# Block 1: other PSUM banks for values, gates and the second half of the heads, convolution taps moved out of the k and v tiles; block 2: five score banks in the second layer, output weights of the last head moved

## What is computed

```
def first_block(x, ...):
    h = rms_norm(x, norm1_g)
    glu_in, q, k, v, gate_logits = jnp.split(h @ w_in, SPLITS, axis=-1)
    a_val, a_gate = jnp.split(glu_in, 2, axis=-1)
    a = causal_depthwise_conv(a_val * sigmoid(a_gate), conv_w, conv_b)      # 31 taps
    y_a = silu(rms_norm(a, conv_norm_g)) @ w_conv_out
    q, k = rms_norm per head, q * HEAD_DIM ** -0.5
    o = attention over three dilated windows, mixed by their lse             # per head
    g_a, g_b = split(sigmoid(gate_logits + gate_b))
    x = x + (g_a * y_a + g_b * (o @ w_attn_out)) @ w_out
    u_val, u_gate = split(causal_depthwise_conv(rms_norm(x, norm2_g) @ w_up, ffn_conv_w, ffn_conv_b))
    return x + (silu(u_gate) * u_val) @ w_down

def second_block(x, ...):        # layer a, then layer b
    y = dsa_mixer(x, ...)            # top-k sparse attention with an index, rope, silu gate
    x = layer_norm(ALPHA * x + y)
    y = stick_breaking_mixer(x, ...) # attention weights from a cumulative log product, silu gate
    return layer_norm(ALPHA * x + y)
```

## Time and profile before

| what | value |
|---|---|
| time, median of 3 runs | 1525.65 us (1523.75 to 1526.76) |
| the profiled execution | 1525.49 us, of which its span is 1523.7 us |
| PE busy | 1484.3 us, 97% of the span |
| DVE, ACT, POOL busy | 1068.1, 752.8 and 572.9 us (70%, 49%, 38%) |
| mean granted clock of PE | 0.996 of full speed |
| HBM traffic | 94 GB/s over the span |

### The profile page before, as it was taken

One profiled execution on the slowest core, in us unless ns is written; L12 is line 12 of the kernel. 1 busy time (PEld: TensorE's weight loads), 2 busy tenths in 40 slices (PEclk: granted clock), 3 DMA queues, 4 the chain that ended last, 5 costly groups with the idle time before them and its releaser, 6 DMA issues.

```text
span 1523.7 us, 19634 instructions
## 1 busy us (share of the span) xinstructions
PE 1484.3 (97%) x7070; PEld 1239.2 (81%) x7070; DVE 1068.1 (70%) x1858; ACT 752.8 (49%) x1490; POOL 572.9 (38%) x453
## 2 busy tenths in 40 slices
PE   9999999899999999999999999999998999999998
PEld 8788887787878888888888788878887888888886
DVE  6847689888955567727745646997997451877975
ACT  6566633665263444424423444346776234566750
POOL 2733347664331111111121111565554355444342
PEclk9999999999999999999999999999999999999999
DMA  6455314642234333333333255366662436545522
GB/s 230 119 158 141 108 56 131 166 133 67 85 95 157 95 111 97 98 96 97 97 97 93 82 154 148 111 177 153 163 162 80 166 114 172 156 113 137 137 81 115
DMA packets 74049, 188.58 MB, mean 124 GB/s; under 512 B 10720, under 2 KB 16224, under 8 KB 73696
## 3 DMA queue, kind: packets, MB, share of 16 engines
q1 hardware_dynamic: 73952, 187.33, 43.3%
HBM read 137.48 MB, written 6.29 MB: 94 GB/s over the span
## 4 chain that ended last, share of the span: by engine, by line
PE 80%; DVE 14%; ACT 4%; issue 1%; POOL 1%; DMA 0%; DVEq 0%; SPq 0%; POOLq 0%; ACTq 0%
PE bank L697 18%; PE bank L699 18%; PE bank L698 18%; PE bank L710 5%; PE bank L712 5%; PE bank L711 5%; DVE bank L1326 2%; PE bank L739 2%; DVE p L1315 2%; PE bank L728 2%; PE bank L747 1%; PE bank L729 1%; PE bank L746 1%; ACT p L1137 1%; DVE ptl L1262 1%
## 5 line engine op out<-in xcount | busy, mean ns | idle before, releaser
L1730 POOL TENSOR_TENSOR wlo<-raw,whi 128x512 fp32r<-128x512 f32 x325 | 438.6, 1358 | 866.1 <-ACT whi L949 865.7
L697 PE MATMUL bank<-xh,whi 128*128 128x512 f32 x1000 | 397.6, 398 | 1.9 <-ACT gb L1041 1.9
L949 ACT ACTIVATE whi<-raw 128x512 fp32r<-128x512 f32 x466 | 281.1, 621 | 222.8 <-PE bank L699 140.9
L699 PE MATMUL bank<-xh,wlo 128*128 128x512 f32 x1000 | 390.9, 391 | 0.0
L698 PE MATMUL bank<-xl,whi 128*128 128x512 f32 x1000 | 390.2, 390 | 0.0
L699 PEld LDWEIGHTS bank<-xh,wlo 128*128 128x128 f32 x1000 | 188.0, 188 | 41.1
L697 PEld LDWEIGHTS bank<-xh,whi 128*128 128x128 f32 x1000 | 188.0, 188 | 38.5 <-ACT gb L1041 2.1
L698 PEld LDWEIGHTS bank<-xl,whi 128*128 128x128 f32 x1000 | 188.4, 188 | 37.1 <-issue 0.5
L1326 DVE SCALAR_TENSOR_TENSOR bank<-cbuf,vec,bank 128x512 f32<-128x512 f32 x240 | 164.3, 746 | 20.1 <-ACT bank L974 10.6
L710 PE MATMUL bank<-whi,xh 128*128 128x512 f32 x340 | 135.3, 398 | 3.6 <-DVE ptl L1262 1.5
L711 PE MATMUL bank<-wlo,xh 128*128 128x512 f32 x344 | 134.7, 392 | 0.0
(11 more groups left out here) (251 smaller groups left out, 2660.2 us busy)
## 6 DMA issues: line engine op xcount, KB each, us to landing
raw<-wst SPq DMA_DIRECT2D x224, 512.0 KB, 3.6
stack<-tmpr SPq DMA_DIRECT2D x152, 128.0 KB, 2.4
stack<-fresh SPq DMA_DIRECT2D x64, 128.0 KB, 2.3
stack<-turnr SPq DMA_DIRECT2D x40, 128.0 KB, 2.4
u<-bias SPq DMA_DIRECT2D x16, 256.0 KB, 2.9
rows<-scratch SPq DMA_DIRECT2D x8, 512.0 KB, 8.5
raw<-wst SPq DMA_DIRECT2D x8, 384.0 KB, 3.1
xr<-xt SPq DMA_DIRECT2D x8, 256.5 KB, 5.8
```

The lines of the kernel that those rows point to most:

```text
L697: e.matmul(bank[:, :], h[:, c], a, start=g + i == 0, stop=False)
L699: m = e.matmul(bank[:, :], l[:, c], a, start=False, stop=g + i == nk - 1)
L949: e.activation(whi[k % NHL][:, 0:n], raw[u % NRAW][:, c:c + n], ACT.Copy).then_inc(*WHI.tick(k))
L1730: e.tensor_tensor(wlo[k % NHL][:, 0:n], raw[u % NRAW][:, c:c + n], whi[k % NHL][:, 0:n].bitcast(F32), ALU.subtract).then_inc(*WLP.tick(k))
```

## The change

Block 1. `PK0` and `PK4` move the transposes Pk0 one step later among the first v tiles and Pk4 one step earlier among the second ones. A table `FIXED` takes the place of the rings for the fourth tile of v0, for q1, k1, v1, the gates 9 to 15 and 0 and for Pq6, Pk6, Pq7, Pk7. `conv_plan` gives no tap to the steps of v1 until Pk4, so that 15 taps come later; from there on the later pairs end and start later as well: the copies out of pair 2,3 and the start of pair 4,5 move from the last v1 tile and gate 8 to gates 10, and 16 more taps than before are still to be done when the first `ao` tile begins. In the steps of k1 and v1 the taps stand behind the step's other work on DVE.

Block 2. The transposes of head 15 take the banks of head 14's, the output tiles take other banks, and the fourth output tile's first piece moves behind head 15's transposes. In layer b scores and transposes share five banks (2, 3, 4, 5, 7) instead of four, and the tiles of q, k and gates two (0, 1) instead of three.

```
-PQ0, PK0, PQ4, PK4 = 2, 4, 3, 6
+PQ0, PK0, PQ4, PK4 = 2, 5, 3, 5
...
-SCORE_BANKS = {"": ((4, 2, 3), (4, 2, 3)), "a": ((2, 3, 4, 5, 7), (2, 3, 4, 5, 7)), "b": ((2, 3, 4, 5), (2, 3, 4, 5))}
-TILE_BANKS = {"a": (0, 1), "b": (0, 1, 7)}
+SCORE_BANKS = {"": ((4, 2, 3), (4, 2, 3)), "a": ((2, 3, 4, 5, 7), (2, 3, 4, 5, 7)), "b": ((2, 3, 4, 5, 7), (2, 3, 4, 5, 7))}
+TILE_BANKS = {"a": (0, 1), "b": (0, 1)}
...
+        o0[3:8] = o0[4:7] + o0[3:4] + o0[7:8]
...
+FIXED = {("v0", 3): 0, ("gate", 9): 0, ("Pq", 6): 1, ("gate", 10): 0, ("Pk", 6): 1, ("gate", 11): 1, ("Pq", 7): 0, ("gate", 12): 1,
+         ("Pk", 7): 0, ("gate", 13): 0, ("gate", 14): 1, ("gate", 15): 0, ("gate", 0): 1, **{(name, tb): b for name, bs in (("q1", (0, 1, 4, 2)), ("k1", (3, 6, 0, 1)), ("v1", (4, 2, 3, 6)))
+                         for tb, b in enumerate(bs)}}
...
+            if name[0] == "T" and len(name) == 2 and x[1] == HEADS - 1:
+
+                bank[x] = bank[name, HEADS - 2, x[2]]
+                continue
...
-                used = [bank.get((t, 15, u)) for u in range(3)] + [bank[g, 7]]
-                if None in used:
-                    r = SCORE_BANKS[x[0][1]][0]
-                    used[:3] = [r[(heads + u) % len(r)] for u in range(3)]
+                used = [bank[t, HEADS - 2, u] for u in range(3)] + [bank[g, 7]]
...
+            quota = 0 if second_pairs <= i < PLAN.index(("Pk", 4)) else quota
...
-            for n in CONV_AT.get(step, ()):
-                conv_tap(n)
+
+            if name not in ("k1", "v1"):
+                for n in CONV_AT.get(step, ()):
+                    conv_tap(n)
...
+            if name in ("k1", "v1"):
+                for n in CONV_AT.get(step, ()):
+                    conv_tap(n)
```

More of the change, by code:

```diff
@@ L335, in banks_in_order @@
             now, ring, n = want, rings[want], 0
+        if key in FIXED:
+            bank[key] = FIXED[key]
+            continue
         bank[key] = ring[n % len(ring)]
@@ L350, in conv_plan @@
     first, second = PLAN.index(("q1", 0, 0, 4)), PLAN.index(("gate", GATES[0], 0))
-    third = PLAN.index(("ao", 0, 0))
+    third, second_pairs = PLAN.index(("ao", 0, 0)), PLAN.index(("v1", 0, 0, 4))
     at, n = {}, 0
```

## The result

| | time, us |
|---|---|
| before | 1526.20 median of 4 runs (1523.75 to 1527.19) |
| changed | 1514.65 median of 4 runs (1511.68 to 1515.82) |
| ratio | 0.9925, 95% interval 0.9912 to 0.9937 |
| predicted | 1511.5, range 1507.5 to 1519 |
| profiled execution of the changed kernel | 1513.99, its span 1512.2 |

The change makes the kernel 0.75% faster, 11.5 us by the medians and 11.5 us by the two profiled executions. The forecast was 14.0 us. So direction and range held, and the forecast was 2.5 us too large. The page of the changed kernel answers to the earlier trace rows: PE does the same work in a shorter span, and the chain that ended last is PE's and VectorE's as before.

The account below looks back on a forecast made before the run. The prediction took PE, busy 97% of the span, as the bound, with only idle and low-clock time to win. Place terms of 12.6 us, restarts 0.8 and small gaps 0.6 made 14.0: 1525.5 to 1511.5 us, range 1507.5 to 1519.

Parts of the forecast that it names:

- where the taps go: Gates 10 and 11 and the convolution's sums: deferred taps cost 0.15 of wait and 0.2 of delay, together -0.35 us.
- both waits go: Head 0: with v0's fourth tile in bank 0, waits of 1.30 and 1.20 us go; 2.5 us gained.
- (b): Pk4: without nine taps the k scales end at 250.2, ahead of Pk4's turn at 252.6; 1.94 us gained.
- (e): Pk5: its 0.34 us wait behind ScalarE's two copies of the finished convolution pair goes, as they move to gate 10.
- (f): Gate 9: its 1.85 us wait for a bank shrinks to 0.3 with bank 0; 1.55 us gained.
- (d): S8,0: its 0.95 us wait for k's stack goes, as 9.0 us of PE work covers 8.8 from Pk4.
- (h): T8: waits 2.0 us (0.9 to 2.9) for GpSimd's scaling of head 8, 1.0 more than before; the new limiter.
- (c): Behind Pk4's wait, 262 to 266 us: the granted clock of 0.57 goes with that wait; 1.7 us gained.
- (g): Around T8, 283 to 287 us: the second stretch of granted clock at 0.57 goes; 1.3 us gained.
- Rival (1): Heads 8 on: waits go but the clock falls once, at T8; costs 1.3 to 1.7 us, giving 1513; chance 0.20.
- the prediction's own sign of being wrong: Wrong if sum(1) waits microseconds for DVE, k scales end after Pk4's turn, or the clock is low where it was not.
- Rival (3): At sum(1): 16 deferred taps push the convolution's sums; at 1.75 us a tap +16.5 us, 1528; chance 0.03.

Follow-up runs that it names:

- the moved load: The changed kernel with one 512 KB weight load issued behind the first four of Pk4's stack copies instead of ahead of them; 1517.22 us, ratio 0.9939.
- the banks alone: The kernel before with only layer b's banks changed: five for scores and transposes, two for the tiles; 1526.33 us, ratio 1.0002.
- the stretch alone: The kernel before with only the heads 8 on part: banks of q1, k1, v1 and gates, taps out of v1, Pk4 one step earlier; 1520.54 us, ratio 0.9955.
- the front alone: The kernel before with only v0's fourth tile in bank 0 and Pk0 one step later; 1524.92 us, ratio 0.9993.
- the first four experiments: The first four follow-ups, whose ratios are to the kernel before at 1526.89 us (29 runs).
- head 8's scaling: The changed kernel with one weight load behind Pk4's copies, and head 8's reciprocal and GpSimd's scaling one step earlier; 1514.72 us, ratio 0.9928.
- the last one: The changed kernel with six taps pulled forward, sum(1) and head 8's GpSimd scaling earlier, a weight load later, variance ahead of a low piece; 1510.66 us, ratio 0.9899.

## Why the prediction was right, and where it was off

The direction, the range and most of the waits were right. That the total came within 2.5 us of the forecast is partly luck: in the trace, places forecast too high (head 0, the heads from 8 on, the taps) and a fall of the clock that no term had come to 4.9 us, and 2.2 us that no term had either came in at Sa0,1. Gains by place, with the prediction's eight restarts and 0.6 us of small gaps put where they belong:

| place | forecast, us | measured, us |
|---|---|---|
| head 0 | 2.7 | 1.3 |
| head 7 | 0.6 | 0.4 |
| heads 8 on, to T8 | 7.65 | 6.7 |
| T8 to spread(1), where the taps go | -0.35 | -1.8 |
| Sa0,1 | nothing | 2.2 |
| fall of the clock in layer a | nothing | -1.1 |
| the rest of block 2 | 3.4 | 3.8 |
| sum | 14.0 | 11.5 |

- **Head 0.** The step "both waits go" holds for bank 4. What was missed is who is late next: the prediction watched only the first gate tile and its bank, and not S0,1, which waited 0.38 for a low part of v on the same VectorE.
- **Head 7.** The wait is 0.6 shorter (0.91 for 1.51), as forecast; 0.4 of it is left between the two rows of the table.
- **Heads 8 on.** (b) holds: Pk4 had no wait; the scales ended at 252.8 instead of 250.2, near the bound, and Pk4 stood at 254.16. (e) and (f) hold: Pk5 and gate 9 have no wait. **(d) failed**: "9.0 covers 8.8" took the copies' time for fixed. PE's own work from Pk4 to S8,0 is 9.0 us, as worked out (262.92 - 253.92 with the moved load), but with Pk4 earlier the copies ran into the weight loads: 11.65 us from Pk4 to S8,0, with 5.2 us for a copy where 2.4 had been. This cost 1.0 us at T8. With the moved load the stretch gives 84.9 - 77.2 = 7.7 us, the sum that was forecast. (h), T8 with 2.0 us, was not to be seen in this trace, but 2.05, 1.74, 2.05 and 2.05 us stood there in the four executions in which S8,0 waited less than 1 us. So T8 was the limiter that (h) named: of 2.9 us won back at S8,0, 1.2 arrived behind T8.
- **The clock** ((c) 1.7 and (g) 1.3 us) was a cost in name only. The two falls stood inside the waits for the copies and for the scaling: without them PE waited 2.55 at S8,0 and 2.26 at T8 in the same code, and came to T8 after the same 84.9 us. The sum comes out all the same, since (d) and (h) were worked out with the falls taken off, so that 0.95 + 1.7 is the wait for the copies and 0.96 + 1.3 that for the scaling. What failed is the reading that a fall seen behind a wait is a price of its own, and that it goes with the wait.
- **Where the taps go** (0.35 of loss): 1.5 at sum(1) and spread(1), 0.2 ahead of them. The adds ended one piece of work too late (0.63 of wait), as the upper bound had it. spread(1)'s doubled wait was not in the sum at all. It comes from VectorE's queue, in which the deferred taps push two low parts of weights ahead of the variance: it started at 428.37, over 2 us behind the end of sum(1) (426.23). With the taps given back it came 0.5 us behind that end and spread(1) waited 0.76; with the variance ahead of the low piece, taps deferred, spread(1) didn't wait.
- **Block 2.** The output tiles of layer a gave 1.8 us, the heads of layer b 1.6, the end 0.3. The two edits were costed as independent; the banks alone gave nothing.
- Rival (1), the waits go and the clock still falls, is what happened, and the prediction's own sign of being wrong, a low clock in stretches where it was not, came true at 266 and at 1152 us. The rival had the place and the price wrong: at T8, 2.05 us of wait were followed by a granted clock of 1.00 in the stretch alone; the fall behind S8,0 was mostly hidden, and the one in layer a cost 1.1 to 1.6. The Trainium skill, "TensorE: Matmul & The Clock Gate" (A second HAM failure mode: psum-queue depth-cycling), tells of short idles between groups that make the clock swing. The traces agree in that each fall ahead of the last 20 us stands at a wait of 1.4 to 3 us, and not in that every such wait has one; the counts are in the section on the hardware.
- Rival (3), slower through the taps, fell: taps took 0.748 us each in the changed kernel as they had 0.746.

## What to carry to other kernels

When a wait is removed ahead of a chain that another engine sets, ask first where PE meets that chain: here T8 met GpSimd's scaling and spread(1) a queue on VectorE, and of the gains in front of them less than half arrived at T8 and nothing that could be told behind spread(1), until the chain itself was moved. Ask also what a fall of the clock hides in: if PE would have waited for another engine anyway, the fall is free, and taking it away wins nothing. A copy's time read from a trace holds only for the traffic it was read in; moving its source earlier moves it into other loads. And look at what stands in an in-order queue ahead of the one small instruction that others wait for: moving a 0.15 us variance ahead of a stalled low part brought more than pulling six taps forward.

## What the runs showed of the hardware

Falls of the clock are not tied to one place. Waits of about 2 us or more stood at the same instructions in many executions, and the clock fell behind them in some and not in others: behind Sa14,2 (2.0 us) in 5 of 14 traces, behind Sa0,1 (2.46) in 3 of 9, behind T8 (2.0 to 2.3) in 2 of 6, behind Pk4 (1.9 to 2.8) in 3 of 5, behind S8,0 (2.4 to 3.0) in 4 of 4, behind spread(1) (2.4) in 2 of 2. A fall took 1.7 us of clock each time but once, when it lasted twice as long. What it cost PE is told by the next rows: nothing where PE then waited for another engine (the two of the kernel before), 1.2 to 1.3 us behind spread(1), 1.6 behind T8 in the front alone and behind Sa0,1. In layer b's banks alone it fell three times, 272 to 277, 1029 to 1034 and 1163 to 1168, each at 0.66 over 5 us, that is at half speed (1.2 GHz) for most of them:

```profile
272.00:277.00 5.00, 5.00 (x20) 4.08 (x19) 3.31 (x10) 3.50 (x7) 2.54 (x2) 0.66 0.37 80
1029.00:1034.00 5.00, 5.00 (x19) 3.99 (x17) 1.93 (x11) 2.33 (x9) 0.00 (x0) 0.66 0.48 132
1163.00:1168.00 5.00, 4.98 (x16) 4.09 (x17) 3.74 (x11) 2.45 (x10) 1.28 (x1) 0.66 0.00 0
```

The times of the kernel before spread by more than one fall. Its 29 runs beside the first four experiments lie in four groups, near 1523.5, 1525.4, 1527.0 and 1529.2 us, with gaps of about 1 us between: steps of 1.6 to 2.2 us. It is tempting to call each step one more fall, but each run has its mean granted clock on record (to 0.001), where one fall of 1.7 us is 0.0011, and the lower three groups don't differ that way: 0.9958, 0.9965 and 0.9966 in the mean. Only the slowest group has a lower clock (0.9942). So the first two steps are something else, or falls that hide in one group and not in another; since only one execution of each kernel has a trace, it stays open. What does follow is that a single trace can be 2 us off its median for no reason of the code, and that a part worth 1 us is to be read from where PE stands and not from the time.

A second such thing is Sa0,1. The code of block 2 ahead of it is the same in all kernels, and its wait was either 2.45 to 2.46 us (before, and eight experiments) or 0.30 and less (the changed kernel, the front, the stretch, head 8's scaling and the last one). The last low part of turned values (`turnr`) that VectorE makes ahead of it took 0.67 us in the five traces with the short wait, and 1.26 to 1.52 in the nine with the long one. It has two inputs in SBUF, like the scales of k that took 1.7 beside GpSimd. So 2.2 of the 11.5 us in the table are a meeting of VectorE with another engine, most likely GpSimd, that came out well in this execution; what decides it stays open.

Both explain why the kernel with the moved weight load, 1.2 us ahead at T8, has a later end in its trace (1516.1 against 1512.2): it waited 2.46 us at Sa0,1, and the clock was low there for two falls' worth (3.5 us of clock over 1015 to 1030) and fell again behind 1156. Whether its median of 1517.22 is more than that, five runs can't tell.
